# Expert stages: slot table sent once, weighted results scattered to token rows, contiguous combine

## The reference

```python
def moe_ffn(h, w_router, b_router, w_e_gate, w_e_up, w_e_down, w_sh_gate, w_sh_up, w_sh_down):
    scores = jax.nn.sigmoid(jnp.matmul(h, w_router, preferred_element_type=jnp.float32))
    _, idx = lax.top_k(scores + b_router.astype(jnp.float32), TOP_K_2)
    wts = jnp.take_along_axis(scores, idx, axis=-1)
    wts = (wts / jnp.sum(wts, -1, keepdims=True) * ROUTE_SCALE).astype(h.dtype)
    ...
    def expert_block(acc, blk):
        tok, wt, e = blk
        yb = swiglu(h_pad[tok], w_e_gate[e], w_e_up[e], w_e_down[e]) * wt[:, None]
        return acc.at[tok].add(yb), None
    ...
    return swiglu(h, w_sh_gate, w_sh_up, w_sh_down) + routed[:n]
```

## Time and profile before

| | us |
|---|---|
| median of 3 runs | 2825.07 |
| lowest, highest run | 2775.64, 2826.87 |
| profiled execution | 2809.68 |
| its span, first to last instruction | 2807.9 |
| PE busy | 2187.5 (78%) |
| DVE busy | 884.4 (31%) |
| ACT busy | 517.4 (18%) |
| POOL busy | 166.8 (6%) |

### The profile page before, as it was taken

How to read it: one execution, slowest core, us unless ns; L and a number is a source line. 1 busy time by engine, 2 the same in 40 slices (tenths; PEclk the granted TensorE clock), 3 DMA queues, 4 the chain that set the end, 5 groups by cost and what they waited for, 6 DMA issues and landing times.

```text
span 2807.9 us, 32157 instructions
## 1 busy us (share of the span) xinstructions
PE 2187.5 (78%) x13040; PEld 1454.2 (52%) x13040; DVE 884.4 (31%) x1790; ACT 517.4 (18%) x957; POOL 166.8 (6%) x177
## 2 busy tenths in 40 slices
PE   3998876688843989977779997788888878888650
PEld 2886665554423865854456675444444444444220
DVE  2134343322224151146642122322222222222227
ACT  2233201100002240236641102011111111111000
POOL 0000000100010000001000000100000000000014
PEclk7997688699986985999999997888998889889775
DMA  6455335499972120111102111477888887778566
GB/s 251 180 225 195 120 118 231 189 420 420 422 300 86 46 86 0 46 75 58 34 16 90 60 60 75 182 264 292 307 324 313 326 331 298 289 287 340 179 227 223
DMA packets 117279, 560.69 MB, mean 200 GB/s; under 512 B 21507, under 2 KB 22531, under 8 KB 65158
## 3 DMA queue, kind: packets, MB, share of 16 engines
q1 hardware_dynamic: 61296, 435.97, 40.3%
q0 software_dynamic: 25552, 70.55, 7.4%
q10 hardware_dynamic: 30278, 51.96, 5.2%
HBM read 512.00 MB, written 71.04 MB: 208 GB/s over the span
## 4 chain that ended last, share of the span: by engine, by line
PE 62%; DMA 13%; DVE 11%; ACT 6%; issue 4%; ACTq 3%; POOL 1%; SPq 0%; DVEq 0%; POOLq 0%
PE ps L242 28%; PE ps L1369 11%; PE ps L1439 8%; DMA y_rows<-arena 6%; DMA arena<-in_egu 4%; ACTq L1487 2%; ACT arena L2417 2%; DVE arena L2453 2%; PE ps L1338 2%; PE ps L1681 1%; DVE pb L1301 1%; DMA arena<-y_rows,arena 1%; PE ps L393 1%; ACT arena L260 1%; ACT arena L2428 1%
## 5 line engine op out<-in xcount | busy, mean ns | idle before, releaser
L1369 PE MATMUL ps<-arena 128*64 128x256 f32 x3904 | 466.5, 395 | 21.1 <-DMA arena<-in_egu 14.9
L1369 PEld LDWEIGHTS ps<-arena 128*64 128x64 f32 x3904 | 298.5, 144 | 235.7 <-issue 94.9
L242 PE MATMUL ps<-arena 128*128 128x256 f32 (+5 forms) x1372 | 362.0, 430 | 23.2 <-DMA arena<-in_sg 7.1
L1439 PE MATMUL ps<-arena 128*64 128x512 f32 x976 | 303.2, 763 | 47.4 <-issue 27.4
L242 PEld LDWEIGHTS ps<-arena 128*128 128x128 f32 (+1 forms) x1372 | 256.3, 216 | 124.5 <-issue 93.4
L1479 DVE COPY arena<-ps 128x512 f32<-128x512 f32 x96 | 66.4, 692 | 370.1 <-PE ps L1439 226.2
L1439 PEld LDWEIGHTS ps<-arena 128*64 128x64 f32 x976 | 77.5, 164 | 174.5 <-issue 174.2
L242 PE MATMUL ps<-tid,pb 128*128 128x2 f32 x348 | 58.6, 272 | 139.7 <-DVE pb L1301 129.4
L1418 DVE TENSOR_TENSOR arena<-arena,ps 128x256 f32<-128x256 f32 (+1 forms) x96 | 36.1, 377 | 406.4 <-ACT arena L1413 406.4
L1327 POOL DMA_INDIRECT arena<-h_rows,arena x80 | 79.4, 993 | 948.1 <-DVE arena L1310 848.7
L242 PEld LDWEIGHTS ps<-tid,pb 128*128 128x128 f32 x348 | 52.2, 214 | 160.9 <-DVE pb L1301 141.4
(11 more groups left out here) (357 smaller groups left out, 3053.4 us busy)
## 6 DMA issues: line engine op xcount, KB each, us to landing
arena<-in_egu SPq DMA_DIRECT2D x206, 1024.0 KB, 18.9
arena<-in_ed SPq DMA_DIRECT2D x103, 1024.0 KB, 6.1
arena<-in_ada SPq DMA_DIRECT2D x48, 1024.0 KB, 7.1
y_rows<-arena ACTq DMA_DIRECT2D x320, 128.0 KB, 6.9
arena<-in_win SPq DMA_DIRECT2D x33, 1024.0 KB, 4.9
y_rows<-arena POOLq DMA_DIRECT2D x1, 15872.0 KB, 64.9
arena<-in_wout SPq DMA_DIRECT2D x8, 1024.0 KB, 6.9
arena<-in_nabias POOLq DMA_DIRECT2D x16, 512.0 KB, 3.9
```

What stands on the lines that cost most here:

```text
L242: z = pe.matmul(o, l, r, start=start and i == 0, stop=stop and i == len(pairs) - 1, skip_group_check=check)
L1369: z = pe.matmul(b[64 * j:64 * j + 64, o:o + 256], X(k), wk(k)[:, j * 256:j * 256 + 256], start=k == 0, stop=k == 7, tile_position=(0, 64 * j))
L1439: z = pe.matmul(b[64 * h:64 * h + 64, :], T[:, s * 128 + 64 * j:s * 128 + 64 * j + 64], wv[:, j, h * 512:h * 512 + 512], start=j == 0, sto ...
```

## The change

The slot numbers are computed ahead of the loop and sent once. `dve_sent` prepares, for every token and choice, a record of four floats: token number, the two row numbers of its result halves, and (later) its weight. `pool_fill` fills a table in HBM (`slots`) with 16384, out of every bound; `pool_send` writes the records to their global slots, one indirect write of 128 x 16 bytes for each tile and choice (8 and 32). `act_slots` loads the table by block, `dve_slots` arranges it, `pe_slots` turns it, and it becomes columns of indices (`ints`) and weights (`scale`) for all blocks. Masks, `tid`, `pb` and the small matmuls are gone, in the further loop too, where six short copies (`dve_block`) shift the columns. The global slots are computed before the loop (in `dve_dispatch`); in stage two `pe_dispatch` and `dve_dispatch` stand ahead of the shared expert.

The results are multiplied by the weight in the copies out of PSUM and written by POOL with indirect writes (`pool_out`, 512 columns each; one per expert in stage one, two in stage two) to the row of their token and choice. In `act_down` and `dve_down` the wait is for the write of the same half of e-2. The combine then loads contiguous rows (`sp_combine`, by SP: 4 loads of 1 MB, 8 of 2 MB) and adds without a factor. `pool_zero` is gone. `sp_more` no longer waits for the first gather. `pe_down_half` puts the parts of a row so that a bank holds 128 half rows.

```diff
-        def pool_zero(pool, w):
-            w.wait_ge(*hg.to("gated", 3))
-            pool.memset(ZR, 0.0).then_inc(*zr.up("pool", "ZR"))
-            w.wait_ge(*zr.to("ZR"))
-            w.wait_ge(*ada.to("mod", 23))
-            pool.dma_start(Y1[32:47].rearrange("a s d -> s a d"), bc(ZR[0:64, :].unsqueeze(1), [64, 15, 1024])).then_inc(
-                *zr.up("rows", "rows", 0, by=16))
-            pool.dma_start(Y2[64:95].rearrange("a s d -> s a d"), bc(ZR.unsqueeze(1), [128, 31, 1024])).then_inc(
-                *zr.up("rows", "rows", 1, by=16))
-
-
...
+        def dve_sent(dve, w, x):
+
+            st, K, c = x.st, x.K, cut(x.cols, 3)
+            w.wait_ge(*ld.to(*ROWS))
+            dve.memset(x.fill, NONE).then_inc(*st.up("dve", "fill"))
+            for t in range(4):
+                dve.tensor_scalar(c[:, 0, t:t + 1], eidx[:, 64:65], 128.0 * t, None, ALU.add).then_inc(*st.up("dve", "c0", t))
+                dve.tensor_scalar(c[:, 1, t:t + 1], eidx[:, 64:65], 2.0 * K, 256.0 * K * t, ALU.mult, ALU.add).then_inc(
+                    *st.up("dve", "c1", t))
+                dve.tensor_scalar(c[:, 2, t:t + 1], eidx[:, 64:65], 2.0 * K, 256.0 * K * t + 1, ALU.mult, ALU.add).then_inc(
+                    *st.up("dve", "c2", t))
+            w.wait_ge(*st.to("c2", 3))
+            for t in range(4):
+                for f in range(3):
+                    dve.tensor_scalar(x.sent[:, t, :, f], iotas[:, 0:K], 2.0 if f else 0.0, c[:, f, t:t + 1], ALU.mult,
+                                      ALU.add).then_inc(*st.up("dve", "sent", t, f))
 
...
                 dve.max(x.g8[:, t, :], x.G[:, t, :]).then_inc(*st.up("dve", "g8", t))
             w.wait_ge(*st.to("g8", 3))
             dve.tensor_copy(x.gi, x.g8).then_inc(*st.up("dve", "gi"))
-            dve.tensor_scalar(x.gs, x.g8, -float(E * B), None, ALU.add).then_inc(*st.up("dve", "gs"))
-            dve.tensor_scalar(x.junk, x.ce, eidx[:, 64:65], None, ALU.is_le, ALU.add, accum_out=x.oe).then_inc(*st.up("dve", "oe"))
-            dve.tensor_copy(x.nov[0:1, :], x.ce[0:1, E - 1:E]).then_inc(*st.up("dve", "nov"))
-            w.wait_ge(*st.to("oeT"))
-            dve.tensor_scalar(x.tab[0:1, :], banks.of(st, "oe").ap[0:1, 0:128], float(E - 1), None, ALU.min).then_inc(
-                *st.up("dve", "tab"))
+            w.wait_ge(*st.to("sent", 3, 2))
             for t in range(4):
                 for k in range(K):
-                    if t or k:
-                        w.wait_ge(*st.to("w8", *((t, k - 1) if k else (t - 1, K - 1))))
-                    dve.scalar_tensor_tensor(x.junk, x.G[:, t, :], x.g8[:, t, k:k + 1], x.weights[:, t, :], ALU.is_equal, ALU.mult,
-                                             accum_out=x.w8[:, t, k:k + 1]).then_inc(*st.up("dve", "w8", t, k))
...
+        def pool_fill(pool, w, x):
+            w.wait_ge(*x.st.to("fill"))
+            n = 4 * x.B
+            pool.dma_start(x.slots_d.rearrange("(b s) f -> b (s f)", s=x.B), x.fill[0:x.N, 0:n]).then_inc(
+                *x.st.up("filled", "filled", by=16))
+
+        def pool_send(pool, w, x):
+            w.wait_ge(*x.st.to("filled"))
+            w.wait_ge(*x.st.to("gi"))
+            for n in range(4 * x.K):
+                t, k = n // x.K, n % x.K
+                w.wait_ge(*x.st.to("w8", n))
+                pool.indirect_dma_start(x.slots_d, bass.IndirectOffsetOnAxis(ap=x.gi[:, t, k:k + 1], axis=0),
+                                        x.sent[:, t, k, :], None).then_inc(*x.st.up("sent", "landed", n, by=16))
+
+        def act_slots(act, w, x):
+
+            w.wait_ge(*x.st.to("landed", 4 * x.K - 1))
+            d = x.slots_d
+            act.dma_start(x.by_block, d.rearrange("(b s) f -> b s f", s=x.B)).then_inc(*x.st.up("table", "table", 0, by=16))
+            if x.B == 64:
+                act.dma_start(x.by_unit, d[0:x.E * 64].rearrange("(b s) f -> b s f", s=128)).then_inc(
+                    *x.st.up("table", "table", 1, by=16))
+
...
+        def dve_slots(dve, w, x):
+
+            T, N, v = cut(x.turned, 5), x.N, x.by_block
+            w.wait_ge(*x.st.to("table", 1 if x.B == 64 else 0))
...
+                dve.tensor_copy(T[0:N, 0, :], v[:, :, 0]).then_inc(*x.st.up("dve", "part", 0))
+                dve.tensor_copy(T[0:N, 1, :], v[:, :, 1]).then_inc(*x.st.up("dve", "part", 1))
+                dve.tensor_copy(T[0:N, 3, :], v[:, :, 3]).then_inc(*x.st.up("dve", "part", 2))
+                for h in range(2):
+                    o = slice(64 * h, 64 * h + 64)
+                    i = slice(64 - 64 * h, 128 - 64 * h)
+                    dve.tensor_copy(T[0:N, 2, o], v[:, i, 2]).then_inc(*x.st.up("dve", "part", 3 + 2 * h))
+                    dve.tensor_copy(T[0:N, 4, o], v[:, i, 3]).then_inc(*x.st.up("dve", "part", 4 + 2 * h))
+            w.wait_ge(*x.st.to("turned"))
+            b = banks.of(x.st, "turned").ap
+            if x.B == 64:
+                dve.tensor_copy(x.unit, b[:, 3 * N:3 * N + x.U]).then_inc(*x.st.up("dve", "unit"))
...
+        def pe_slots(pe, w, x):
+            b = banks.turn(x.st, ("turned",), ("scale",))
+            for f in b.free:
+                w.wait_ge(*f)
+            w.wait_ge(*x.st.to("part", 7 if x.B == 64 else 6))
+            o = 0
+            for v, n in table_parts(x):
+                z = pe.transpose(b.ap[:, o:o + n], v, ident[0:n, 0:n])
+                o += n
+            z.then_inc(*x.st.up("pe", "turned"))
+            b = banks.turn(x.st, ("oe",), ("tab",))
             for f in b.free:
                 w.wait_ge(*f)
             w.wait_ge(*x.st.to("oe"))
             pe.transpose(b.ap[0:1, 0:128], x.oe, ident).then_inc(*x.st.up("pe", "oeT"))
 
-
-        def dve_number(dve, w, x, u):
-            st, per, P = x.st, x.per, PB[u % 2]
-            w.wait_ge(*st.to("posm"))
-            if u >= 2:
-                w.wait_ge(*st.to("ni", u - 2))
-            dve.tensor_tensor(P.rearrange("p t (j s) -> p t j s", j=per),
-                              bc(iota128[:, 0:x.B].unsqueeze(1).unsqueeze(1), [128, 4, per, x.B]),
-                              bc(x.posm[:, :, per * u:per * u + per].unsqueeze(3), [128, 4, per, x.B]),
-                              ALU.is_equal).then_inc(*st.up("dve", "P", u))
-
-        def dve_index(dve, w, x, u):
...
+        def pool_clear(pool, w, x, n0, n1):
+            for u in range(n0, n1):
+                pool.memset(XG[u], 0.0).then_inc(*x.st.up("pool", "clear", u))
...
             if u < NX:
-                pool.memset(XG[u % NX], 0.0).then_inc(*x.st.up("pool", "clear", u))
                 w.wait_ge(*x.st.to("clear", u))
             else:
                 w.wait_ge(*x.st.to("xt", u - NX, 1))
-            w.wait_ge(*x.st.to("idx", u))
-            pool.indirect_dma_start(XG[u % NX], None, x.H, bass.IndirectOffsetOnAxis(ap=IDX[u % NX], axis=0),
+            w.wait_ge(*x.st.to("unit" if x.B == 64 else "ints"))
...
-        def act_out(act, w, x, e):
-            if x.B == 128:
-                w.wait_ge(*x.st.to("y", e, 0))
-            w.wait_ge(*x.st.to("y", e, 1))
-            Y = YB[e % 2]
-            for s, h in y_parts(x):
-                act.dma_start(x.Y[e][64 * s:64 * s + 64, 512 * h:512 * h + 512],
-                              Y[64 * h:64 * h + 64, 512 * s:512 * s + 512]).then_inc(*x.st.up(f"yo{e % 2}", "yo", e, s, h, by=16))
+                w.wait_ge(*x.st.to("yo", e - 2, h))
+            dve.tensor_scalar(YB[e % 2][:, 512 * h:512 * h + 512], banks.of(x.st, "d", e, h).ap, x.scale[:, h, e:e + 1], None,
+                              ALU.mult).then_inc(*x.st.up("dve", "y", e, h))
+
+        def pool_out(pool, w, x, e):
+
+            w.wait_ge(*x.st.to("ints"))
+            for h in range(x.banks):
+                w.wait_ge(*x.st.to("y", e, h))
+                pool.indirect_dma_start(x.rows_d, bass.IndirectOffsetOnAxis(ap=x.ints[:, 1 + h, e:e + 1], axis=0),
+                                        YB[e % 2][:, 512 * h:512 * h + 512], None, bounds_check=1024 * x.K - 1,
+                                        oob_is_err=False).then_inc(*x.st.up(f"yo{e % 2}{h}", "yo", e, h, by=16))
 
         BX, BG, BY = [0, 1], [3, 4], [6, 7]
 
...
-                pe_number(pe, w, x, u)
             pe_xrows(pe, w, x, 0)
             for e in range(x.E + 1):
                 if e < x.E:
...
-                if 0 <= e - 1 < x.E:
+                if e:
                     act_down(act, w, x, e - 1)
-                if 0 <= e - 2 < x.E:
-                    act_out(act, w, x, e - 2)
 
         def dve_experts(dve, w, x):
-            for u in range(NX):
-                dve_number(dve, w, x, u)
-                dve_index(dve, w, x, u)
+            dve_slots(dve, w, x)
             dve_xrows(dve, w, x, 0)
...
         def pool_experts(pool, w, x):
-            for u in range(x.U):
+            for u in range(NX):
                 pool_gather(pool, w, x, u)
+            for e in range(x.E):
+                if e % x.per == 0 and e // x.per + NX < x.U:
```

(70 more changed lines are left out.)

317 lines of the change are left out of this document (131 added, 186 removed).

## The result

| | before | after |
|---|---|---|
| median of the runs, first comparison | 2820.5 us (4 runs) | 2630.5 us (4 runs) |
| ratio, 95% interval | | 0.940 (0.925 to 0.956) |
| median, second comparison | 2800.3 us (11 runs) | 2604.4 us (6 runs) |
| ratio, 95% interval | | 0.9315 (0.926 to 0.937) |
| the profiled execution | 2809.7 us, span 2807.9 | 2613.4 us, span 2611.5 |

The account below looks back on a forecast made before the run. It took weight DMA to bound the first expert stage and TensorE's waits for masks and `y_rows` writes the second. Terms of -184 us from 2809.68 gave 2626; it said 2630 us, range 2575 to 2740.

Parts of the forecast that it names:

- the sum: Whole kernel, all stretches added: 0 - 6 - 156 - 6 + 1 - 17 = -184 us, giving 2626 us.
- The loop's rate: Second expert loop, first to last gate: 63 x 7.66 + 26 x (3.76 + 2.07) = 634 us, against 802.
- The 5.83 us for a large block: Second expert loop: each of 26 large blocks adds 3.76 us in the gate and 2.07 in the down product.
- The 8 us for stretches of small blocks that outrun their weights: Second expert loop: allowance of 8 us for late weights, raising 634 us to 642 us.
- The start: Start of second loop: serial chain of counts, ranks, 32 sends, table and gather; first gate about 1805 us, against 1800.
- Indirect writes: POOL's sends and result writes: between 0.93 and 1.93 us each to issue, 0.95 us taken for a send.
- First stage and its combine: First expert stage: net 0, from -8 to +12 us; its combine, with four 1 MB loads issued together: -6 us.
- Tail: From the second loop's last gate to the first product of the further blocks, 29.3 us before: -6 us.
- Further blocks: Five further blocks after the second loop: mask chain replaced by six short copies, +1 us, up to 10 if writes land late.
- Combine: Second stage's combine to the end: 66 to 68 us instead of 84, set by DVE, -17 us.
- DMA as the bound: Rival, second loop: DMA gets no more than 307 GB/s, last gate 86 us later, 2716 us; chance 0.18.
- GpSimd as the bound: Rival: scattered writes make POOL the limit; gain gone at 4.8 us a write, 3020 us at 6; chance 0.08.

Follow-up runs that it names:

- the kernel with both edits: The kernel before, with masks built an iteration ahead and result writes issued by GpSimd as soon as copied: second loop 646.4 us, ratio 0.946 to before.

## Why the prediction was right

- **What bounds the kernel.** Right in the order (DMA in stage one, waits in stage two). The waits told the causes, but not their prices: the wait for masks, 103.2 us in the earlier trace rows, was worth more than its own length, since it also slowed the products behind it; the waits on `y_rows`, 342.9 us on two engines, were worth 29 alone.
- **Luck in the total.** 2630.5 against 2630 us is closer than the sum was. Its span was 12 us off, the loop 20 us too long and its start 17 too short, 15 of them from a standstill that came in three of nine executions; and the second comparison has 2604 us. The range and the mechanism are what held.
- **The loop's rate.** Taken from iterations of the old trace without numbering and stall, and so right whatever the causes were, as far as those iterations were free of them. 63 x 7.66 held. The 5.83 us for a large block did not: now 11.12 - 7.67 = 3.45 for its gate and 12.68 - 11.12 = 1.56 for its down product, 5.01. 26 x 0.82 = 21 us, nearly the whole difference of the term (predicted 642, measured 622.4). It is not the clock: in the two intervals that gave 11.42 and 9.73 it was 1.00 (columns as in the earlier trace rows):

```profile
2569.82:2581.24 11.42, 10.09 (x84) 6.15 (x82) 2.14 (x4) 1.58 (x3) 0.00 (x0) 1.00 1.01 422
2581.24:2590.97 9.73, 8.34 (x60) 4.50 (x58) 2.04 (x4) 1.50 (x3) 0.00 (x0) 1.00 0.94 341
```

The second still held a piece of the cost to be removed. ScalarE was issuing four `y_rows` writes when the gate's SiLU fell due:

```profile
2582.92 2.44 ACTq L1487 DMA_DIRECT2D y_rows<-arena  x4
2585.40 0.38 ACT L1413 ACTIVATE arena<-ps 128x256 f32<-128x256 f32 x1 [1.97 <-PE ps L1426]
```

That is 4.16 us behind the gate's start at 2581.24; in the changed kernel, in the same kind of iteration, the SiLU comes 3.67 us behind it (2415.48 to 2419.15). These 0.49 us are the difference between 9.73 and 9.24. The prediction said of this issuing that it is "partly in the 7.66 already"; it was in the price of the large block. In the first of the two, the down product starts 0.31 us later than in the changed kernel, and the trace doesn't show why. So the 21 us are 13 of ScalarE's issuing and 8 of open cause. The 8 us for stretches of small blocks that outrun their weights have the right size and fall in the right place: 63 x 7.67 + 26 x 5.01 = 613.5 leaves 8.9 us, and the long intervals close rows of small blocks, 8.13, 9.50 and 8.52 us after two of 9.23 and 7.67, 9.77 after 9.24 and 7.76. The gates at the end of the 9.50 and the 9.77 waited 1.58 and 1.93 us; the profile names VectorE's result copy for the first and nothing for the second. That both waited for weights is likely, not shown, as their landings aren't on record.
- **The start.** The chain's own time was right: 70.8 us against 69. Sends 1.26 us apart (1.25), started at 1725.6, not 1741: the counts and ranks came earlier, which was given back in the table, 11.6 us where the sum had 4, with the weights ahead of it. In the profiled execution another 15 us were the standstill. The sum named no such hazard; "the shared expert hides the sending" is true for 30 of the 40 us.
- **Indirect writes.** Between the ends 0.93 and 1.93 us, the value taken held: 0.96 for 16 bytes a row, 1.00 for 2 KB. The rule of the Trainium skill, "SBUF — State Buffer", section "Who interferes with whom", would have made the sends beside VectorE's work longer. The longest of the 32 took 1.04 us, the median 0.96, but this is hardly a test: only the first five lie beside VectorE's work. The Trainium skill, "DMA: Bandwidth & Descriptors", specifications, has small elements written by read-modify-write; the landing of 16-byte rows was 2.1 us on idle queues, less than the 2.4 us of the quickest scattered write of 2 KB rows, so no price of it is seen.
- **First stage and its combine.** -11.7 to the shared expert, predicted -6. First gate 561.6 (568 said); last gate 801.85 against 804.95, -3.1 for the 0. From there to the combine's square 32.0 us against 38.0 (833.81, and 842.98 in the earlier trace rows), the -6 of the sum. The last 2.5 us lie between there and the shared expert, in work that wasn't changed.
- **The ends.** Tail -7.1 (-6). Further blocks -6.4 where the sum had +1: the old writes landed 6.5 us after their issue and the new ones 2.6, and the later iterations are 15.43 us apart, before 15.55 to 17.23. Part of this is luck: the sixteen gate products took 8.83 us in three of the five old blocks and in one of the five new ones, 7.1 to 7.9 in the others. Combine -12.4 for -17: the term "7 us to the first load" was too short. Four loads of 2 MB are in flight at once:

```profile
2540.00 13.66 DMA arena<-rowsb
2553.68 2.31 DVE arena L2703
```

```profile
2548.37 2.29 DVE L2703 TENSOR_TENSOR arena<-arena 128x2048 f32<-128x2048 f32 x1 [14.19 <-DMA arena<-rowsb]
```

VectorE starts 8.75 us after the issue at 2539.62. The adds of a load held (4.75 us, predicted 4.8). What is left of the 71.9 us, the work per token tile and the tail, took 25 us where the sum had 20.
- **The rivals.** DMA as the bound: refuted at its 307 GB/s: the loop ran at 359, share 0.91, with at most the few us above that weights may have cost; the kernel with both edits ran its loop at 382 GB/s. GpSimd as the bound: refuted in price (1.00 us a write, break-even 4.8). But doubling its writes brought 56 us, by a mechanism that was not among the rivals.

## What to carry over

Read the rate of a loop from iterations of its own trace that lack the cost in question, and check on every engine that they lack it: the row for a large block still had ScalarE issuing the old writes, and 26 times half a microsecond came of it. Before restructuring a loop, ask where in its order the waited-for instruction stands; here one mask an iteration earlier was worth 87 us alone, and with the writes issued in time 156. Waits that stand one behind the other have no prices of their own: taking one makes the next grow (199 to 356 us on ScalarE), so estimate them together and test both. Where a load is slow behind a queue of weights, moving it ahead only passes the queue on to the next transfer of the chain, unless the weights wait for that one too. And when one execution shows a stall that others don't, count what its trace lacks before giving the stall a cause.

## What the runs showed of the hardware

- In traced executions, TensorE's signals arrived late, in bunches, while GpSimd issued long trains of indirect transfers: 24 bunches, in iterations that were 54 us longer together, with five transfers per iteration; one bunch of 0.5 us in the thirteen loops with three at most. The products' own records were not late. The stalls beside 32 sends came only in traces that lack about a tenth of TensorE's signals, so the recording isn't ruled out as their cause. A train is not sufficient (six of nine trains of 32 beside the shared expert, and 192 sends in the attention, disturbed nothing), and what makes the difference is open: size, number in flight or coincidence weren't separated.
- The same down products took 601, 753 and 794 ns in three loops with granted clocks of 1.00, 0.92 and 0.89. 86.9 us of waiting in front of them came with another 57 us of slower products.
- Scattered writes of 128 rows: 0.96 to 1.00 us of GpSimd for 16 bytes as for 2 KB a row, landing 2.1 to 2.6 us on idle queues; behind loads 6.7 us for a last send, and 4.3 to 7.9 for the results' writes.
